# A shared ninth round for two groups of tokens in a mixture-of-experts stage, and one round of weight loads fewer

## The reference, cut to what matters

```python
top_p, top_i = lax.top_k(jax.nn.softmax(le, axis=-1), TOP_K)        # TOP_K = 2
experts = (g_sel[:, None] * EXPERTS_PER_GROUP + top_i)
...
hid = jax.nn.silu(xblk @ w_gate[e]) * (xblk @ w_up[e])              # 1024 -> 512
return hid @ w_down[e]                                              # 512 -> 1024
```

## Time and profile before

| What | Value |
|---|---|
| Time, median of 3 runs | 2282.05 us (2282.0 to 2282.59) |
| The profiled execution's own time | 2283.39 us, its span 2281.7 us |
| TensorE busy | 2093.5 us, 92% of the span |
| 16 DMA engines, 400 to 760 us | 101% busy by the records, 421 GB/s |
| Loads of `moe_w` | 204 of 1 MB, 17 rounds |

### The profile page before, as it was taken

One profiled execution on the slowest core, in us unless ns is written; L12 is line 12 of the kernel. 1 busy time (PEld: TensorE's weight loads), 2 busy tenths in 40 slices (PEclk: granted clock), 3 DMA queues, 4 the chain that ended last, 5 costly groups with the idle time before them and its releaser, 6 DMA issues.

```text
span 2281.7 us, 26227 instructions
## 1 busy us (share of the span) xinstructions
PE 2093.5 (92%) x10354; PEld 1555.0 (68%) x10354; DVE 905.9 (40%) x1168; ACT 667.4 (29%) x851; POOL 381.2 (17%) x364
## 2 busy tenths in 40 slices
PE   6997968777787779999999999999999999999998
PEld 5895833232232348888777888877889987888887
DVE  5536340000000026777754333336766234333332
ACT  3434211100101016666533221223222423221222
POOL 0000320000000004545521100102444001100100
PEclk9998979999999999999999999999999999999999
DMA  5230379999999971111212222232222322222220
GB/s 206 78 108 1 122 303 420 421 421 421 421 421 421 421 324 67 64 56 59 91 44 93 92 92 92 92 111 92 83 87 91 130 93 77 98 102 92 92 92 37
DMA packets 57658, 378.13 MB, mean 166 GB/s; under 512 B 8960, under 2 KB 9056, under 8 KB 13920
## 3 DMA queue, kind: packets, MB, share of 16 engines
q1 hardware_dynamic: 51120, 363.04, 40.6%
q0 software_dynamic: 6448, 13.82, 1.6%
HBM read 371.01 MB, written 15.26 MB: 169 GB/s over the span
## 4 chain that ended last, share of the span: by engine, by line
PE 67%; DMA 18%; DVE 7%; issue 5%; ACT 2%; SPq 0%; POOL 0%; DVEq 0%; POOLq 0%
PE bank L578 19%; PE bank L580 19%; PE bank L579 19%; DMA moe_w<-weights_in 17%; PE bank L840 3%; PE bank L863 2%; DVE o_tmp L2330 1%; DVE k_dec L2306 1%; PE bank L936 1%; PE bank L1259 1%; PE bank L706 1%; PE bank L1037 1%; PE bank L1049 1%; DVE ws L2315 0%; PE bank L1207 0%
## 5 line engine op out<-in xcount | busy, mean ns | idle before, releaser
L578 PE MATMUL bank<-u_hi,w_hi 128*128 128x512 f32 x1152 | 464.7, 403 | 0.7 <-issue 0.7
L580 PE MATMUL bank<-u_hi,w_lo 128*128 128x512 f32 x1152 | 456.6, 396 | 0.0
L579 PE MATMUL bank<-u_lo,w_hi 128*128 128x512 f32 x1152 | 456.4, 396 | 0.0
L1808 DVE TENSOR_TENSOR w_lo<-raw,w_hi 128x2048 fp32r<-128x2048 f32 x96 | 232.6, 2423 | 301.6 <-ACT w_hi L1310 301.3
L840 PE MATMUL bank<-moe_w,xe 128*64 128x512 f32 x1088 | 266.9, 640 | 90.0 <-DMA moe_w<-weights_in 86.3
L840 PEld LDWEIGHTS bank<-moe_w,xe 128*64 128x64 f32 x1088 | 92.7, 146 | 263.3 <-issue 263.1
L1310 ACT ACTIVATE w_hi<-raw 128x2048 fp32r<-128x2048 f32 x96 | 183.6, 1912 | 273.8 <-PE bank L580 272.8
L578 PEld LDWEIGHTS bank<-u_hi,w_hi 128*128 128x128 f32 x1152 | 217.2, 189 | 53.9 <-issue 3.5
L579 PEld LDWEIGHTS bank<-u_lo,w_hi 128*128 128x128 f32 x1152 | 217.4, 189 | 53.1 <-issue 2.4
L580 PEld LDWEIGHTS bank<-u_hi,w_lo 128*128 128x128 f32 x1152 | 217.1, 188 | 52.8
L578 PE MATMUL bank<-w_hi,u_hi 128*128 128x256 f32 (+1 forms) x640 | 192.4, 301 | 6.8 <-issue 6.8
(11 more groups left out here) (434 smaller groups left out, 2800.4 us busy)
## 6 DMA issues: line engine op xcount, KB each, us to landing
moe_w<-weights_in SPq DMA_DIRECT2D x204, 1024.0 KB, 25.1
raw<-weights_in SPq DMA_DIRECT2D x128, 1024.0 KB, 4.8
y_pairs<-pair_rows SPq DMA_DIRECT2D x4, 1024.0 KB, 7.8
res<-x_in SPq DMA_DIRECT2D x1, 2048.0 KB, 7.8
token_rows<-xn POOLq DMA_DIRECT2D x4, 512.0 KB, 3.4
v_rows<-vals SPq DMA_DIRECT2D x2, 1024.0 KB, 4.3
vals<-v_rows SPq DMA_DIRECT2D x2, 1024.0 KB, 8.0
out<-out_tile SPq DMA_DIRECT2D x4, 512.0 KB, 2.6
```

The lines of the kernel that those rows point to most:

```text
L578: nc.tensor.matmul(out_ap, a_hi, b_hi, start=first, stop=False)
L579: nc.tensor.matmul(out_ap, a_hi, b_lo, start=False, stop=False)
L580: return nc.tensor.matmul(out_ap, a_lo, b_hi, start=False, stop=last)
L1808: nc.vector.tensor_tensor(w_lo[:, n % 2], raw[:, n % RAW], w_hi[:, n % 2].bitcast(F32), ALU.subtract) \
```

## The change

The extra round and its 12 loads are dropped. Its group of tokens, now only those beyond 64 of one chosen pair, is served in round 9 (`SHARED` = 8, counted from 0) with that pair's own weights.

- **Which pair.** VectorE finds the pair with the fullest expert among pairs 2 to 15 (`is_shared`), swaps it with pair 8 in the order of service and writes the order to `order_int`; the slots and scales of the two pairs are swapped too (`by_round_seat`). The rows for the table are worked out with the shared pair's overflow first (`first_lift`), and only what is left goes to the general loop (`n_general`), which has 16 places instead of 14.
- **SyncE** waits once for `order_int` and reads one number of it at the start of each round (`value_load`).
- **TensorE, ScalarE, VectorE** run rounds 0 to 7 in a loop, then the shared round as straight code (group A up, group B up, A down, B down), then rounds 9 to 14 in a second loop, then round 15. In the shared round only group B's matmuls count `unit_used`; those of group A count another semaphore, `shared_done`.
- **GpSimd** gathers a group before it waits for an older group's result instead of after it.

The diff, cut to its core:

```diff
             with sp.Fori(1, NPAIR) as i:
+                first_unit = sp.value_load(order_int[0:1, bass.ds(i, 1)]) * PAIR_UNITS + U_MOE
...
-            sp.wait_ge(dest_ready, 1)
-            over_unit = [sp.value_load(over_int[0:1, b:b + 1]) * PER_EXPERT + U_MOE for b in range(2)]
-            for j in range(PER_EXPERT):
-                for b in range(2):
-                    s = 2 * j + b
-                    sp.wait_ge(unit_used, U_EXTRA - PAIR_UNITS + s + 1)
-                    sp.dma_start(moe_w[s][:], weights_in[bass.ds(over_unit[b] + j, 1)].rearrange("u p n -> p (u n)")) \
-                        .then_inc(raw_landed[s], 16)
...
-            with pe.Fori(0, NPAIR // 2) as i:
+            with pe.Fori(0, SHARED // 2) as i:
                 for b in range(2):
-                    expert_round(i * 2 + b, (1 - b, i * 16 + 16 * (b + 1)))
-            expert_round(EXTRA, None)
+                    expert_round(i * 2 + b, i * 2 + b, (1 - b, i * 16 + 16 * (b + 1)))
+            tokens_there(SHARED)
+            up_units(SHARED, shared_done, 4)
+            turn_next(1, 16 * (EXTRA // 2 + 1))
+            turn_back(SHARED)
+            tokens_there(EXTRA)
+            up_units(SHARED)
+            turn_next(0, 16 * (EXTRA // 2 + 2))
+            hidden_there(SHARED)
+            down_units(SHARED, shared_done, 4)
+            turn_back(EXTRA)
+            hidden_there(EXTRA)
+            down_units(SHARED)
+            with pe.Fori(0, (GROUPS - EXTRA) // 2 - 1) as i:
+                for b in range(2):
+                    expert_round(i * 2 + (EXTRA + 1 + b), i * 2 + (EXTRA + b), (1 - b, i * 16 + 16 * (EXTRA // 2 + 2 + b)))
+            expert_round(GROUPS - 1, NPAIR - 1, None)
...
-            for e in range(ROUNDS):
+            for e in range(GROUPS):
+                if e + 2 < GROUPS:
+                    pool.wait_ge(xe_turned, e + 1)
+                    gather(e + 2)
                 pool.wait_ge(y_left, e + 1)
                 pool.wait_ge(y_right, e + 1)
...
-                if e + 2 < ROUNDS:
-                    pool.wait_ge(xe_turned, e + 1)
-                    gather(e + 2)
```

More of the change, by code:

```diff
@@ L246, in build @@
         in_pair = tiny("in_pair", [2 * TB, NPAIR])
+        fullest, order_f = tiny("fullest", [NPAIR]), tiny("order_f", [NPAIR])
+        is_shared, shared_experts = tiny("is_shared", [NPAIR]), tiny("shared_experts", [NE])
+        order_int = tiny("order_int", [NPAIR], I32)
+        by_pair_seat, by_round_seat, moved = [tiny(name, [3, NPAIR]) for name in ("by_pair_seat", "by_round_seat", "moved")]
+        first_limit, first_lift = tiny("first_limit", [NE]), tiny("first_lift", [NE])
+        n_general = tiny("n_general", [NE])
         seat = tiny("seat", [2 * TB])
@@ L841, in up_units @@
                                                   start=c == 0, stop=c == KC - 1)
-                            if k == 3:
-                                mm.then_inc(unit_used, 1)
+                            if k == 3 and (step == 1 or (j % 2 == 1 and b == 1)):
+                                mm.then_inc(done, 1)
             def turn_hidden():
@@ L864, in down_units, with turn_next @@
                                                       start=c == 0, stop=c == 3)
-                                if k == 1 and half == 1:
-                                    mm.then_inc(unit_used, 1)
+                                if k == 1 and half == 1 and (step == 1 or (j == 5 and b == 1)):
+                                    mm.then_inc(done, 1)
             pe.wait_ge(x_gathered[0], 16)
             turn_rows(0)
-            def expert_round(e, next_rows):
+            def turn_next(b, landed):
+                pe.wait_ge(x_gathered[b], landed)
+                turn_rows(b)
@@ L1468, in expert_round, with result_left @@
                     .then_inc(hid_t_left, 1)
+            def result_left(b, y_from, counted, count):
                 act.wait_ge(y_free[b], y_from)
-                act.wait_ge(unit_used, u0 + 12)
+                act.wait_ge(counted, count)
                 nc.scalar.activation(y_rows[:, b, 0:512], bank[5][:], ACT.Copy).then_inc(y_left, 1)
-            with act.Fori(0, NPAIR // 2) as i:
+            def expert_round(e, u0, b, y_from, last, scale):
+                gate_rows(unit_used, u0 + 4, scale)
+                if not last:
+                    next_tokens(e + 1)
+                hidden_left(e)
+                result_left(b, y_from, unit_used, u0 + 12)
+            with act.Fori(0, SHARED // 2) as i:
                 for b in range(2):
@@ new lines, in _ @@
+            late_pairs = slice(2, NPAIR)
+            chain(nc.vector.memset(is_shared[:, 0:2], 0.0))
+            chain(nc.vector.tensor_reduce(fullest[:], count.rearrange("p (g l) -> p g l", l=2), AX.X, ALU.max))
+            chain(nc.vector.tensor_reduce(best[:, 7, 0:1], fullest[:, late_pairs], AX.X, ALU.max))
+            chain(nc.vector.tensor_tensor(fullest[:, late_pairs], fullest[:, late_pairs],
+                                          best[:, 7, 0:1].to_broadcast([P, NPAIR - 2]), ALU.is_equal))
@@ new lines, in _ @@
+            chain(nc.vector.tensor_tensor(by_round_seat[:], by_round_seat[:], by_pair_seat[:], ALU.add))
+            chain(nc.vector.tensor_tensor(moved[:], by_pair_seat[:], spread, ALU.mult))
+            chain(nc.vector.tensor_reduce(by_round_seat[:, :, SHARED], moved[:], AX.X, ALU.add))
+            nc.vector.tensor_scalar(slots[:, :, 2:], by_round_seat[:, 0:2, 2:], float(NO_PAIR), None, ALU.add).then_inc(slots_ready, 1)
+            nc.vector.tensor_copy(slot_scale[:], by_round_seat[:, 2]).then_inc(slots_ready, 1)
@@ L2185, in expert_round, with result_right @@
                     .then_inc(hid_t_right, 1)
+            def result_right(b, y_from, counted, count):
                 dve.wait_ge(y_free[b], y_from)
-                dve.wait_ge(unit_used, u0 + 12)
+                dve.wait_ge(counted, count)
                 nc.vector.tensor_copy(y_rows[:, b, 512:1024], bank[6][:]).then_inc(y_right, 1)
-            with dve.Fori(0, NPAIR // 2) as i:
+            def expert_round(e, u0, b, y_from, last, scale):
+                gated_rows(e, unit_used, u0 + 8, scale)
+                if not last:
+                    next_tokens(e + 1)
+                hidden_right(e)
+                result_right(b, y_from, unit_used, u0 + 12)
+            with dve.Fori(0, SHARED // 2) as i:
                 for b in range(2):
```

168 lines of the change are left out of this document (117 added, 51 removed).

## The result

The changed kernel takes 2260.02 us (median of 4 runs, 2257.98 to 2262.45) where the kernel before takes 2282.2 us: a ratio of 0.9903, 95% interval 0.9891 to 0.9915. In a second series it was 0.9907 (0.9889 to 0.9924; 2261.83 us). The forecast was 2260.5 us. The profiled execution took 2260.41 us with a span of 2258.7 us, 23.0 us less than the span before.

The account below looks back on a forecast made before the run. Load bandwidth was taken to bound the kernel until about 828 us, VectorE's routing chain ahead of the first refill. Terms -29.8 + 3.9 + 3.7 + 0.7 = -21.5 us gave 2260.5 us, range 2255.5 to 2269.

Parts of the forecast that it names:

- The loads: Ring of weight loads: twelve fewer loads, six pairs of units at 4.97 us each, save 29.8 us (bounds -29.8 and -31.1).
- The shared round: Round 9: serving the second group there leaves two holes in the loads, 1.6 and 2.3 us, costing +3.9 us (0 to 16).
- The walk: Step-by-step timing of round 9's landings, products and freed buffers, from which the +3.9 us for the holes was taken.
- T: The landing of round 9's first pair of units, from which the prediction counts its times there.
- rival 2: Second group runs slow in round 9: TensorE's clock at 0.50, hole about 20 us larger, 2280.5 us, no change; chance 0.04.
- Two marks that I set for the prediction being wrong: In the shared round: a PEclk below 1, and one hole of 5 us or more, would show the forecast wrong.
- The routing: VectorE's chain ahead of xe: eleven operations hidden in the wait for seat sums, the other additions cost +3.7 us (+2 to +8.6).
- Rival 4: VectorE's additions are hidden and the first issue isn't later: 2256.8 us; chance 0.05 for a larger gain, this with no hole.
- The end: Last scatter: the last group is now a full one instead of ten rows, +0.7 us (bounds 0 and +3.1).
- At nothing: Parts counted as costing nothing: SyncE's register reads, the wait for order_int, earlier gathers, the skipped general loop.
- Rival 1: Shared round: an engine without instructions at a new seam, 10 us, 2270.5 us; chance 0.10 including another hole up to 12 us.
- Rival 3: General loop runs all 16 trips, 400 us in all, some 2660 us; chance 0.03 including other ways to be slower.

Follow-up runs that it names:

- kernel 1: The kernel before without the extra round's 12 loads and products, its gather and scatter kept (result incomplete): 2251.62 us, ratio 0.9871.
- the repeat: The changed kernel, unedited, measured again in the second series: 2261.83 us, ratio 0.9907 to the kernel before.
- kernel 2: The kernel before with unread small VectorE operations added at three places, like the new routing's: 2284.79 us, ratio 1.0014.
- 7: The changed kernel with group B's 64 gate and up products done twice, the first time counted by nobody: 2272.77 us, ratio 0.996.

## Why the prediction was right

**The loads.** Term -29.8 us, measured -30.1 by kernel 1. That the 1.3 us of gather and scatter stay is not tested by itself: kernel 1 keeps them too.

**The shared round.** Term +3.9 us, measured +4.2 (kernel 1; 4.9 in the repeat). The walk held: B's up began at T+23.65 (forecast T+22.2), its w_down at T+46.9 (T+45.6), the second hole lacks 2.1 us (2.3). A's last 32 products took 9.97 us where the repeat has 8.78; TensorE's granted clock was 0.52 from 566 to 570 us, from within the wait of 3.19 us on. So rival 2's mechanism was there, though in A's products, not B's, and worth 1.2 us against the repeat. Two marks that I set for the prediction being wrong were met, a PEclk below 1 in the shared round and one hole of 5 us or more; the mark of the hole misread the matter. The walk counts from the last landing (581.9 us). Behind that the first hole lacks 2.5 us (1.6 forecast), with the second 4.6 in all. Ahead of it 4.1 us are missing, which the walk knew nothing of. Nor did it know that the hole takes the ring's last lag from 8.1 to 3.5 us, 4.6 less. These two nearly cancel: counting waits on landings came out right without the drift, and that is in part luck.

**The routing.** Term +3.7 us, measured +3.5 (3.8 in kernel 2). The eleven operations were hidden, as said, with 0.86 us to spare (0.6 forecast). Rival 4 is excluded by the first refill, 5.06 us later, of which 1.6 were there already at the row of best.

**The end.** Term +0.7 us, measured +0.5. That isn't shown to be the change's: the same stretch took 16.38 us in the repeat, 0.1 less than before, and its scatter 4.99 us.

**At nothing.** The register reads of SyncE don't show: from the last step of round 8 (550.39) to the first of round 9 (555.36) it is 4.97 us, the pitch of before. Rival 1, a stall for code, isn't seen: in the shared round no wait on TensorE is put down to its instruction issue. The rule of the Trainium skill (Runtime: NRT & Kernel Launch, Instruction fetch mechanics) on a taken branch to a page not held therefore had no visible price at the new seams; whether the pages were held there, no trace shows. Rival 3, the general loop, didn't run.

**What the sum left out.** Two stretches that the change doesn't touch moved by +1.6 and -2.7 us. The +1.6 goes with TensorE's granted clock near 28 us, before, then after:

```profile
28.00:30.00 2.00, 2.00 (x11) 1.63 (x10) 1.82 (x1) 0.39 (x1) 0.00 (x0) 1.00 0.00 0
```

```profile
28.00:30.00 2.00, 2.00 (x6) 1.55 (x5) 1.96 (x1) 0.79 (x1) 0.00 (x0) 0.50 0.00 0
```

It isn't the change's: of ten profiled executions the three with 1.00 from 28 to 32 us (before, 2 and 7, which has the changed routing) reach best at 297.15 to 297.95 us, the other seven at 299.39 to 301.64. The -2.7 is left open. The kernel before has two low stretches, and the changed kernel, which reaches the same code 20.3 us earlier, has 1.00 at both:

```profile
1135.00:1139.00 4.00, 4.00 (x20) 3.65 (x19) 3.52 (x6) 1.01 (x2) 3.62 (x3) 0.61 0.13 18
1155.00:1163.00 8.00, 6.60 (x28) 5.56 (x28) 3.93 (x11) 0.63 (x1) 2.47 (x3) 0.57 0.00 1
```

But kernel 1 has such a stretch at the second place as well (0.53 from 1123 to 1127 us) and took 1434.6 us behind the experts, as little as the changed kernel; the ten executions took 1434.2 to 1436.9. That these shifts came to 1.1 us in favour is luck, and so is part of the closeness of 2260.02 to 2260.5; the ring's terms are known to about 1 us, the total to 1 or 2.

## What to carry to other kernels

In a stage bound by a ring of loads, a pause costs its missing bytes, less what it takes off the lag between the DMA engines, as far as that would have been paid at the ring's end: 3.6 to 4.9 us here, after some 260 us of a full queue. When buffers serve two users, let both use each buffer as it lands (5.4 us here) and not one user after the other. And look at what stands between the last input and the first refill: moving one copy on each of two engines ahead of work that nobody awaits gave 6.1 us of the span.

## What the runs showed of the hardware that wasn't expected

- The DMA engines drift apart in a full queue: the 16 increments of one load came within 0.8 us at 307 us and within 16.6 us at 828 us. A pause sets this back, and it grows again: 8.3 us at 581.9, 0.4 at 587.7, 8.1 at 807.3.
- Low stretches of TensorE's granted clock (0.50 is the lower of its two levels, 1.2 GHz instead of 2.4) come at other places in each execution, also where TensorE is busy all the time; in these rows it had been idle for a part shortly before. It was at 0.52 from 566 to 570 us, around the end of a wait of 3.2 us, and 0.61 at 1135 and 0.57 at 1155 us in the kernel before, where TensorE did nothing from 1131 to 1133 and from 1151 to 1153 us.
- Chained VectorE operations on 16 columns, reading the same operand, follow each other every 0.21 us (2.27 us for eleven), 48 columns every 0.24 us (1.68 for seven).
